# Tile-wise normalisations with the inverse deviation in PSUM, and the mLSTM head norm in one piece, in a fp32 decoder layer

## What is computed

```python
h = layer_norm(alpha * h + 0.5 * swiglu(h, ffn1...), ln1_g, ln1_b)      # norm 0
h = layer_norm(alpha * h + hybrid_mixer(h, ...), ln2_g, ln2_b)          # norm 1
h = layer_norm(alpha * h + 0.5 * swiglu(h, ffn2...), ln3_g, ln3_b)      # by rows, not touched here

# group A of the mixer: top-k selected keys, attention over a shared latent
# group B of the mixer: mLSTM, 4 heads of 128, 512 real tokens
h = num / jnp.maximum(jnp.abs(den), jnp.exp(-m_t))[..., None]
mu = jnp.mean(h, axis=-1, keepdims=True)
var = jnp.mean(jnp.square(h - mu), axis=-1, keepdims=True)
h = (h - mu) * lax.rsqrt(var + LN_EPS) * ml_norm_g
y_ml = jax.nn.sigmoid(o_m) * h                     # output gate, o_m is a projection of x
return concat([y_att, y_ml], axis=-1) @ w_out
```

## Time and profile before

| what | value |
|---|---|
| median of 3 runs | 1118.2 us (1115.24 to 1118.43) |
| the profiled execution | 1114.91 us, its span 1113.0 us |
| PE busy / DVE / ACT / POOL in the span | 97% / 42% / 31% / 12% |
| FFN 1 with its inputs | to about 404 us |
| norm 0 | 404 to 432 us |
| mixer | 432 to 712 us |
| norm 1 | 712 to 738 us |
| FFN 2 and the last norm | 738 to 1113 us |

### The profile page before, as it was taken

One profiled execution on the slowest core, in us unless ns is written; L12 is line 12 of the kernel. 1 busy time (PEld: TensorE's weight loads), 2 busy tenths in 40 slices (PEclk: granted clock), 3 DMA queues, 4 the chain that ended last, 5 costly groups with the idle time before them and its releaser, 6 DMA issues.

```text
span 1113.0 us, 16112 instructions
## 1 busy us (share of the span) xinstructions
PE 1077.5 (97%) x6635; PEld 933.9 (84%) x6635; DVE 466.9 (42%) x731; ACT 345.6 (31%) x452; POOL 129.5 (12%) x95
## 2 busy tenths in 40 slices
PE   8999999999999998999988999989999999999995
PEld 7999999999999997689865568768888888888885
DVE  4332332323232254689885533463232323232326
ACT  3322322222121234534337542353232323221211
POOL 5000000000011115212312103250000000000000
PEclk9999999999999999999998999999999999999998
DMA  6424233231322323122210101222424232143221
GB/s 192 114 76 112 75 93 96 75 101 52 105 79 78 115 76 97 39 77 77 77 38 1 39 1 38 76 76 76 113 75 112 76 109 80 52 142 104 78 78 75
DMA packets 159166, 90.35 MB, mean 81 GB/s; under 512 B 6596, under 2 KB 156792, under 8 KB 159128
## 3 DMA queue, kind: packets, MB, share of 16 engines
q1 hardware_dynamic: 159128, 89.83, 28.3%
HBM read 87.72 MB, written 2.10 MB: 81 GB/s over the span
## 4 chain that ended last, share of the span: by engine, by line
PE 88%; DVE 5%; ACT 3%; POOL 2%; issue 1%; DMA 0%; DVEq 0%; SPq 0%; POOLq 0%
PE ps L911 74%; PE ps L1081 4%; POOL xl L478 2%; PE ps L1355 2%; PE ps L1335 1%; PE ps L1346 1%; DVE x L1601 1%; PE ps L1363 1%; DVE sil L1595 1%; PE ps L1143 1%; ACT whi L606 1%; PE ps L1036 0%; PE ps L1035 0%; DVE x L1584 0%; PE ps L1037 0%
## 5 line engine op out<-in xcount | busy, mean ns | idle before, releaser
L911 PE MATMUL ps<-xl,whi 128*128 128x264 f32 (+1 forms) x1264 | 351.0, 330 | 8.9 <-POOL xl L478 8.0
L911 PE MATMUL ps<-xh,whi 128*128 128x264 f32 (+1 forms) x1264 | 355.8, 331 | 2.7 <-DVE wlo L1439 1.6
L911 PE MATMUL ps<-xh,wlo 128*128 128x264 f32 (+1 forms) x1264 | 352.8, 329 | 0.0
L911 PEld LDWEIGHTS ps<-xl,whi 128*128 128x128 f32 x1264 | 211.7, 189 | 36.4 <-POOL xl L478 16.1
L911 PEld LDWEIGHTS ps<-xh,whi 128*128 128x128 f32 x1264 | 212.5, 189 | 29.4 <-issue 5.2
L911 PEld LDWEIGHTS ps<-xh,wlo 128*128 128x128 f32 x1264 | 213.6, 189 | 22.2 <-issue 0.2
L1430 DVE TENSOR_TENSOR wlo<-wraw,whi 128x2048 fp32r<-128x2048 f32 (+1 forms) x81 | 171.6, 2118 | 144.0 <-ACT whi L606 144.0
L606 ACT ACTIVATE whi<-wraw 128x2048 fp32r<-128x2048 f32 (+1 forms) x89 | 152.4, 1712 | 129.6 <-PE ps L911 123.8
L1463 DVE TENSOR_TENSOR ht<-ps,sil 128x528 f32<-128x528 f32 (+1 forms) x44 | 30.8, 700 | 253.7 <-PE ps L911 247.4
L911 PE MATMUL ps<-hh,whi 128*128 128x264 f32 (+1 forms) x506 | 132.8, 319 | 0.0
L911 PE MATMUL ps<-hl,whi 128*128 128x264 f32 (+1 forms) x506 | 132.5, 318 | 0.0
(11 more groups left out here) (226 smaller groups left out, 921.2 us busy)
## 6 DMA issues: line engine op xcount, KB each, us to landing
wraw<-in_ffn_w_gate SPq DMA_DIRECT2D x44, 512.0 KB, 4.0
wraw<-in_ffn_w_up SPq DMA_DIRECT2D x43, 512.0 KB, 5.2
wraw<-in_ffn_w_down SPq DMA_DIRECT2D x32, 384.0 KB, 3.4
wraw<-in_ffn_w_down SPq DMA_DIRECT2D x32, 320.0 KB, 3.8
wraw<-in_w_in SPq DMA_DIRECT2D x19, 512.0 KB, 4.6
wraw<-in_w_out SPq DMA_DIRECT2D x8, 512.0 KB, 4.0
xin<-in_x SPq DMA_DIRECT2D x2, 1024.0 KB, 5.9
out<-zrow SPq DMA_DIRECT2D x8, 256.0 KB, 2.0
```

The source lines that it names most:

```text
L911: mm = pe.matmul(ps[:, b + e, 0:width], w, mov, start=(first and n == 0), stop=(last and n == 2))
```

## The change

Three edits. First, in `norm` for p = 0 and 1 the reciprocal is written to PSUM bank 6 (and 7), whose mean squares have been read by then, and the 8 multiplications take it from there. Second, the mLSTM norm is made once over all four blocks, where it was made over blocks 1 to 3 and then over block 4: one square root on ACT where there were two. Its normalisations stand as 8 pieces before the first attention scores and 8 after the second, where there were 12 at the end of `mlstm` and 2 + 2 between scores. Third, PE issues the numerators of block 4 between the two halves of the last `o_half`, and ACT copies them before the last sigmoid, with the square root after that sigmoid.

```diff
--- before.py
+++ after.py
@@ -807,12 +807,10 @@
                 copy_num(2)
                 o_out(18)
                 copy_num(3)
-                mlstm_sd(0, 3)
+                copy_num(4)
                 o_out(19)
-                copy_num(4)
+                mlstm_sd()
                 for h in range(ATT_H):
-                    if h == 4:
-                        mlstm_sd(3, 4)
                     act.wait_ge(ql_done, h + 1)
                     act.activation(ql[:, h, N_META:T], ps[:, 4 + h % 4, :], ACT.Copy).then_inc(ql_ready, 1)
                 attention()
@@ -822,10 +820,9 @@
                         hi(MIX0 + LATE_UNITS[m], LATE_UNITS[m] % 2, UW, True)
                 hi(UNIT0[2] + 1, 1, UW, True)
 
-            def mlstm_sd(j0, j1):
-                act.wait_ge(ml_var, 1 if j0 == 0 else 2)
-                v = mls[:, 0, :].rearrange("p (h j) -> p h j", h=ML_H)[:, :, j0:j1]
-                act.activation(v, v, ACT.Sqrt).then_inc(ml_sd, 1)
+            def mlstm_sd():
+                act.wait_ge(ml_var, 1)
+                act.activation(mls[:, 0, :], mls[:, 0, :], ACT.Sqrt).then_inc(ml_sd, 1)
 
             def mlstm_hi(h):
                 act.wait_ge(yml_ready, h + 1)
@@ -1200,8 +1197,9 @@
                 o_half(18, 4, KT)
                 scores(4)
                 numerators(3)
-                o_half(19)
+                o_half(19, 0, 4)
                 numerators(4)
+                o_half(19, 4, KT)
                 lat_queries()
                 attention()
                 for n in range(N_PROJ, MIX_UNITS):
@@ -1592,13 +1590,15 @@
                 centre(0)
                 centre(1)
                 dve.wait_ge(s["sd_done"], 1)
-                dve.reciprocal(var, flat(sil[:, 1, :], p)).then_inc(s["rstd_done"], 1)
+                rstd = bank(6, p)
+                dve.reciprocal(rstd, cols(sil[:, 1, :], p)).then_inc(s["rstd_done"], 1)
                 dve.wait_ge(s["rstd_done"], 1)
                 for k in range(KT):
                     if 2 <= k + 1 < KT:
                         centre(k + 1)
                     dve.wait_ge(s["sub_done"], k + 1)
-                    dve.tensor_tensor(flat(x[:, k, :], p), flat(x[:, k, :], p), var, ALU.mult).then_inc(s["norm_done"], 1)
+                    z = cols(x[:, k, :], p)
+                    dve.tensor_tensor(z, z, rstd, ALU.mult).then_inc(s["norm_done"], 1)
 
             def index_scores():
                 dve.wait_ge(proj_evac, 4)
@@ -1731,43 +1731,39 @@
                 for j, r0, r1 in ((1, 5, 7), (2, 7, 10), (3, 10, 13), (4, 13, TOPK // 8)):
                     weights(j)
                     select(4, r0, r1)
-                mlstm_norm(0, 3)
-                normed_mlstm(range(ML_H), 0, 3)
-                mlstm_norm(3, 4)
-
-            def mlstm_norm(j0, j1):
-                for j in range(j0, j1):
+                mlstm_norm()
+
+            def mlstm_norm():
+                for j in range(4):
                     dve.wait_ge(num_copied, 2 * (j + 1))
                     for h in range(ML_H):
                         dve.bn_stats(bst[:, h * 4 + j, :], nums[:, h, j, 0:ML_DV]).then_inc(dv, 1)
                         n_dv[0] += 1
                 dve.wait_ge(dv, n_dv[0])
-                for h in range(ML_H):
-                    for j in range(j0, j1):
-                        dve.bn_aggr(mv[:, h * 4 + j, :], bst[:, h * 4 + j, :]).then_inc(dv, 1)
-                        n_dv[0] += 1
+                for q in range(ML_H * 4):
+                    dve.bn_aggr(mv[:, q, :], bst[:, q, :]).then_inc(dv, 1)
+                    n_dv[0] += 1
                 dve.wait_ge(dv, n_dv[0])
-                hj = lambda v: v.rearrange("p (h j) -> p h j", h=ML_H)[:, :, j0:j1]
-                em = tok[:, :, :].rearrange("p j e -> p e j")[:, 4:8, 1 + j0:1 + j1]
-                den = nums[:, :, j0:j1, ML_DV]
+                hj = lambda v: v.rearrange("p (h j) -> p h j", h=ML_H)
+                em = tok[:, :, :].rearrange("p j e -> p e j")[:, 4:8, 1:NT]
+                den = nums[:, :, :, ML_DV]
                 link(dve.scalar_tensor_tensor(hj(mls[:, 0, :]), den, -1.0, den, ALU.mult, ALU.max))
                 link(dve.tensor_tensor(hj(mls[:, 0, :]), hj(mls[:, 0, :]), em, ALU.max))
-                link(dve.reciprocal(hj(mls[:, 1, :]), hj(mls[:, 0, :])))
-                link(dve.tensor_tensor(hj(mls[:, 0, :]), hj(mls[:, 1, :]), hj(mls[:, 1, :]), ALU.mult))
-                link(dve.tensor_tensor(hj(mls[:, 0, :]), hj(mls[:, 0, :]), hj(mv[:, :, 1]), ALU.mult))
-                dve.tensor_scalar(hj(mls[:, 0, :]), hj(mls[:, 0, :]), EPS, None, ALU.add).then_inc(ml_var, 1)
-                dve.wait_ge(ml_sd, 1 if j0 == 0 else 2)
-                link(dve.reciprocal(hj(mls[:, 2, :]), hj(mls[:, 0, :])))
-                link(dve.tensor_tensor(hj(mls[:, 2, :]), hj(mls[:, 2, :]), hj(mls[:, 1, :]), ALU.mult))
-
-            def normed_mlstm(heads, j0, j1):
+                link(dve.reciprocal(mls[:, 1, :], mls[:, 0, :]))
+                link(dve.tensor_tensor(mls[:, 0, :], mls[:, 1, :], mls[:, 1, :], ALU.mult))
+                link(dve.tensor_tensor(mls[:, 0, :], mls[:, 0, :], mv[:, :, 1], ALU.mult))
+                dve.tensor_scalar(mls[:, 0, :], mls[:, 0, :], EPS, None, ALU.add).then_inc(ml_var, 1)
+                dve.wait_ge(ml_sd, 1)
+                link(dve.reciprocal(mls[:, 2, :], mls[:, 0, :]))
+                link(dve.tensor_tensor(mls[:, 2, :], mls[:, 2, :], mls[:, 1, :], ALU.mult))
+
+            def normed_mlstm(heads):
                 for h in heads:
-                    for j in range(j0, j1):
+                    for j in range(4):
                         q = h * 4 + j
                         v = nums[:, h, j, 0:ML_DV]
                         ins = dve.tensor_scalar(v, v, mv[:, q, 0:1], mls[:, 2, q:q + 1], ALU.subtract, ALU.mult)
-                    if j1 == 4:
-                        ins.then_inc(hn_ready, 1)
+                    ins.then_inc(hn_ready, 1)
 
             def gated_mlstm(heads):
                 for h in heads:
@@ -1807,6 +1803,7 @@
                     dve.tensor_tensor(xl[:, 0:4, START[j]:END[j]], ps[:, 2, :].rearrange("p (c r) -> p c r", c=4),
                                       xh[:, 0:4, START[j]:END[j]].bitcast(F32), ALU.subtract).then_inc(ya_lo, 1)
 
+                normed_mlstm((0, 1))
                 late = None
                 def copy_even(G, tiles):
                     for i in tiles:
@@ -1823,8 +1820,8 @@
                         if G < GROUPS:
                             for q in (2 * half, 2 * half + 1):
                                 masked(4 * G + q)
-                        if G == 0:
-                            normed_mlstm((2 * half, 2 * half + 1), 3, 4)
+                        if (G, half) == (0, 0):
+                            normed_mlstm((2, 3))
                         if (G, half) in ((0, 1), (1, 0)):
                             gated_mlstm((2 * G, 2 * G + 1))
                         if half == 0:
```

## The result

The changed kernel took 1104.7 us in the median of 4 runs (1102.98 to 1106.45), beside 1117.6 us for the kernel before (4 runs): a ratio of 0.9897, 95% interval 0.9879 to 0.9915. Timed once more on another chip it gave 1105.56 against 1116.59, 0.9899 (0.9882 to 0.9917). The forecast was 1109.6 us, with a range of 1104.5 to 1115.0; the measured median lies 0.2 us inside its lower end. The profiled execution is 1104.67 us, its span 1102.8.

The account below looks back on a forecast made before the run. PE, busy 97% of the span, was taken as the bound, so edits pay only where it waits or runs at its lower clock. Gains 1.9 + 0.7 + 6.0 = 8.6 us, 1118.2 to 1109.6 us, range 1104.5 to 1115.0.

Parts of the forecast that it names:

- (a): Whole kernel: the forecast itself, 7.5 to 9.5 us less; chance 0.55.
- (c): Norms: `wlo` runs behind all POOL pieces, last `xl` 1.7 us earlier still, PE limits to 1.5 each; 1106.6 us; chance 0.12.
- The loop over two tiles in the norms: Norms: DVE with two SBUF operands and POOL exclude each other, 1.785 us per tile; PSUM operand gives 1.45, norm 0 gains 1.9.
- Norm 1: Second norm, by the same steps as norm 0: gain 0.7 us.
- with PE at 737.1 against 737.77: Norm 1: the times of PE after and before the change, behind the 0.7 us gain.
- There POOL already worked without gaps: Norm 1: POOL's pieces already gapless before, 1.86 us each, so less to be had than in norm 0.
- The end of the mLSTM: Latent queries to first `weigh`: PE's 3.1 us stall behind ACT's square root goes; gain taken as 6.0 us.
- The walk at full clock: End of the mLSTM, stepped through with the same durations: gain 6.5 us at full clock, 5.2 if the clock falls.
- The cover of 0.6 us: Before the single square root: ACT's table load ends at 583.1, DVE's statistics chain at 582.5, so the load decides.
- (b): End of the mLSTM gives only half, through the lower clock or a root waiting for DVE; gain 5.6, 1112.6 us; chance 0.22.
- (d): The 3.1 us stall reappears before the first scores, only the norms gain 2.6 us; 1115.6 us; chance 0.08.
- (e): Both norms: DVE's reciprocal write to PSUM is slow, making the kernel slower, 1120 us; chance 0.03.

Follow-up runs that it names:

- e7: The changed kernel with DVE's `wlo` moved behind POOL's last `xl` in both norms; 1104.79 us, ratio 0.9896.
- r1: The kernel before, unchanged, run once more for a second profile; profiled execution 1116.80 us.
- e3: The kernel before with only ACT's order changed: last sigmoid and copy of the last numerators ahead of the first square root; one run, 1118.06 us.
- e5: The kernel before with only the mLSTM norm made in one round, block 4's numerators still behind the whole product; one run, 1113.37 us.
- e1: The kernel before with only the norms' reciprocal written to PSUM and read from there; 1111.41 us, ratio 0.9961.
- e2: The changed kernel with the reciprocal back in SBUF, both mLSTM edits kept; 1110.39 us, ratio 0.9957.
- e4: The kernel before, norm still in two rounds, block 4's numerators between the product's halves, their copy and the last sigmoid before the root; one run, 1117.42 us.
- e6: The changed kernel with three heads normalised before the first attention scores and one later, instead of two and two; 1104.73 us, ratio 0.9897.
- r3: e6 run once more, beside the changed kernel on the same chip; 1103.07 us against 1105.56.

## Why the forecast was right, and where not

The time fell inside the range, and the three mechanisms were there, but the number owes something to luck. The forecast proper, (a) of the prediction, was 7.5 to 9.5 us less (chance 0.55). The medians fell by 11.0 and 12.9 us and the edits' own pieces by 10.7, so (a) was missed. What kept 1104.7 inside the range is its lower end, which had been set for rival (c), and (c)'s mechanism isn't what happened.

**The loop over two tiles in the norms: right.** With one operand in PSUM DVE and POOL no longer exclude each other (0.69 to 0.70 us throughout). The Trainium skill, "SBUF — State Buffer", section "Who interferes with whom", says it as a rule: only a DVE instruction with two SBUF inputs (or in a two-port mode) contends with a GpSimd instruction that reads SBUF, and the lock is exclusive. The trace agrees, and on the blocked side of e7 too: 1.53 us less of POOL when `wlo`, with two SBUF inputs, is moved away. Norm 0 was forecast at 1.9 and gave 2.1; POOL's start was foreseen at 415.8 (415.89), `wlo` at 422.1 (422.13), POOL's end at 429.1 (428.84).

**Norm 1: mis-sized, 0.7 forecast, 2.1 measured.** The failed step is "with PE at 737.1 against 737.77". I took the last wait in the earlier trace rows for that of the last `xl`, as it is in norm 0. It was for the seventh. DVE's and PE's timelines of the kernel before:

```profile
726.97 1.19 DVE L1601 TENSOR_TENSOR x<-x,sil 128x512 f32<-128x512 f32 x1
...
733.21 3.39 DVE L1430 TENSOR_TENSOR wlo<-wraw,whi 128x2048 fp32r<-128x2048 f32 x1
```

```profile
738.35 0.40 PE L911 MATMUL ps<-xh,whi 128*128 128x512 f32 x1
...
739.28 0.63 PE L911 MATMUL ps<-xl,whi 128*128 128x512 f32 x2
```

Four more products of high parts and a further pair with `xl` stand behind 737.77: the last `xl` was used at 739.28. My 737.1 for the last one, set against that, is a gain of 2.2. The sum for the new time was right, what it was subtracted from was not. The reason given for the small gain, "There POOL already worked without gaps", was a misreading too: before, multiplications stretched here as in norm 0 (1.16 to 1.20 us), PE took the second to the sixth `xl` 1.71 us apart, and after the change ACT's pace is 1.41.

**The end of the mLSTM: right, a little small.** The walk at full clock gave 6.5; measured 6.67 to the first `weigh`, 6.50 to norm 1. I wrote 6.0 to allow for the lower clock, which didn't come in either profile. How much of the 6.67 is the clock of the kernel before, r1 shows (PE's timeline):

```profile
587.11 5.44 PE L1312 MATMUL ps<-qa,wuk 64*128 64x512 f32 x16 [3.08 <-ACT upad L780]
...
602.96 2.33 PE L1355 MATMUL ps<-v,cs 16*128 16x512 f32 x4 [1.35 <-DVE v L1818]
```

The wait of 3.08 us is the same, but the clock fell only once before the first `weigh`, which came 23.09 us after the statistics (579.87), 4.86 and not 6.67 more than in the changed kernel. The clock fell again right behind it (604 to 608 us), and M came out the same, 141.61. By this comparison some 1.8 of the 6.5 us are time lost at the lower clock in the kernel before, behind the stall; the rest is the stall, the second root and what they hold up. The cover of 0.6 us before the root was there: DVE's chain ended at 581.97, the table load at 582.53. The Trainium skill, "ScalarE: Activation LUTs", section "What ACT_TABLE_LOAD costs", has 2.66 us for a switch of tables, load and drain together; by that, as an estimate, the root would have stood at about 583.9. The row has the sigmoid's end at 581.23 and the root at 582.54, 1.31 us, and the measurement decides. e3 to e5 show the interaction that the prediction only implied: while two rounds remain, the second root stands ahead of latent queries 5 to 8 whatever precedes it; with one round, it waits for block 4 unless its numerators come early.

**The sum.** Of 8.6 us forecast, the edits' own pieces gave 10.7. Between the two first profiles lie 10.2: 10.7 less 1.5 in A, plus 1.1 in F, less 0.1 at the start. The medians lie 11.0 to 12.9 apart. What this has over 10.7 I put down to the clock: the kernel before has longer PE waits behind which it falls (granted clock 0.991 and 0.989 over the span, 0.994 and 0.993 after). The other executions of the kernel before on record bear this out: three with a granted clock of 0.993 took 1113.9 to 1114.5 us, sixteen with 0.987 or 0.988 took 1115.1 to 1117.3. That the waits are the reason is argued. e1 and e2 gave 4.1 and 5.1 us by their medians, 9.2 together and less than the whole; of e2 the profile shows 1.4 us lost before norm 0 with the clock at its lower level between 16 and 21 us, as in e4 and e5; where that drop lay before 16 us (e3, e6, e7, r3) it cost nothing.

**The rivals.** (a), the forecast itself: too small, as said. (b), half at the mLSTM: no, the clock stayed at 1.00. (c), more than forecast: the total came near its 1106.6, but not by its mechanism. `wlo` did get in behind the fifth piece, and e7 shows that its price was wrong by one step: it left out that PE needs `wlo` itself at once. (d), the stall reappears: not here, but it is what e3 and e4 do. (e), a slow write to PSUM: no, 3.45 us.

## What to carry to other kernels

Where a gain is the difference of two times, check that both are the same event: count the tiles up to the wait in the trace, don't take the last wait for that of the last tile. Two waits in a row for one chain (first round, second round) must go together: edit 3 alone only moved the stall, edit 2 alone gave half. And before moving an operation out of another's way, ask who needs its result next: e7 won 3.65 us and paid 3.06 back.

## What the runs showed of the hardware

The granted clock falls to its lower level for 3.4 or 6.8 us at a time, twice 10.2 (in e3 and e4; added up from stretches of 1 us), not always in the same place for the same kernel. Around 500 us every profile has such a drop; the kernel before once had 3.4 us of it and once 6.8, and that is the 1.6 us between the two levels of A. The two profiles of the kernel before (the first, then r1):

```profile
494.00:498.00 4.00, 4.00 (x24) 2.12 (x24) 3.73 (x13) 3.71 (x4) 1.17 (x1) 1.00 0.00 0
498.00:502.00 4.00, 4.00 (x21) 4.00 (x22) 3.73 (x13) 1.35 (x4) 3.64 (x2) 0.57 0.00 0
502.00:506.00 4.00, 4.00 (x35) 4.00 (x35) 3.76 (x12) 0.45 (x1) 0.00 (x0) 1.00 0.88 263
```

```profile
498.00:502.00 4.00, 4.00 (x13) 2.48 (x12) 3.73 (x13) 2.93 (x6) 3.57 (x1) 0.62 0.00 0
502.00:506.00 4.00, 4.00 (x21) 4.00 (x20) 3.73 (x12) 0.00 (x0) 1.23 (x2) 0.52 0.44 120
```

The loop of FFN 2 runs at one of two levels 1.1 us apart, spread evenly over its units (11.22 and 11.07 us, or 11.27 and 11.13), at full clock, with kernels that differ in nothing there. What sets it stays open. Each is larger than the 0.6 us that e6 gains, which is why medians of four runs don't settle it and the pieces do.
